# A transformer mixer's three branches laid out in a new order: low-rank tile first, fourteen rounds of inverse, heads and gate tiles

## What is computed

```python
h = rms_norm(x, mix_norm[l])
p = h @ w_in[l]
p_rwkv = token_shift(p[..., :SHIFT_COLS], shift_mu[l])
p_fox = p[..., SHIFT_COLS:SHIFT_COLS + FOX_COLS]
gates = jax.nn.sigmoid(p[..., SHIFT_COLS + FOX_COLS:])
gate_a, gate_b = gates[..., :D_MODEL], gates[..., D_MODEL:]
y_a = rwkv7_mixer(p_rwkv, ...) @ rwkv_proj[l]
y_b = fox_mixer(p_fox, ...) @ fox_proj[l]
x = x + (gate_a * y_a + gate_b * y_b) @ w_out[l]
```

## Time and profile before

| | |
|---|---|
| median of 3 runs | 2981.29 us (2980.33 to 2991.32) |
| profiled execution | 2975.66 us, span 2973.9 us |
| TensorE busy | 2758.8 us (93%) |
| VectorE busy | 1886.0 us (63%) |
| ScalarE busy | 1244.0 us (42%) |
| GpSimd busy | 779.5 us (26%) |
| mean granted clock of TensorE | 0.962 of full |

### The profile page before, as it was taken

One profiled execution on the slowest core, in us unless ns is written; L12 is line 12 of the kernel. 1 busy time (PEld: TensorE's weight loads), 2 busy tenths in 40 slices (PEclk: granted clock), 3 DMA queues, 4 the chain that ended last, 5 costly groups with the idle time before them and its releaser, 6 DMA issues.

```text
span 2973.9 us, 43682 instructions
## 1 busy us (share of the span) xinstructions
PE 2758.8 (93%) x17592; PEld 2495.1 (84%) x17592; DVE 1886.0 (63%) x3243; ACT 1244.0 (42%) x1739; POOL 779.5 (26%) x340
## 2 busy tenths in 40 slices
PE   8989999999999988699999999999799857898998
PEld 7869999999888866599999988888798746776896
DVE  5655997776555566659977765555654675415554
ACT  4434453333444444444633344444444512132443
POOL 0000987664000001029966630000000230042000
PEclk9999999999999999899999999999899978889999
DMA  6554554445666643255544455665456410023454
GB/s 203 161 183 148 171 179 151 139 142 160 192 193 191 192 151 113 79 177 175 172 157 138 141 177 191 191 191 191 135 185 191 127 59 24 1 85 104 159 183 144
DMA packets 122888, 449.49 MB, mean 151 GB/s; under 512 B 13712, under 2 KB 13840, under 8 KB 122560
## 3 DMA queue, kind: packets, MB, share of 16 engines
q1 hardware_dynamic: 120800, 439.47, 46.4%
q0 software_dynamic: 1888, 7.23, 0.7%
HBM read 445.60 MB, written 1.05 MB: 150 GB/s over the span
## 4 chain that ended last, share of the span: by engine, by line
PE 82%; DVE 13%; ACT 2%; POOL 2%; issue 1%; DMA 1%; DVEq 0%; SPq 0%; ACTq 0%
PE ps L428 11%; PE ps L429 11%; PE ps L430 11%; PE ps L478 11%; PE ps L480 11%; PE ps L479 10%; DVE W L1294 10%; PE ps L547 4%; PE ps L676 2%; PE ps L450 2%; PE ps L452 2%; PE ps L451 2%; DVE x L1294 1%; POOL lo L1957 1%; PE ps L414 1%
## 5 line engine op out<-in xcount | busy, mean ns | idle before, releaser
L912 ACT ACTIVATE hi<-ring 128x1024 fp32r<-128x1024 f32 x830 | 878.6, 1059 | 1256.6 <-PE ps L430 649.2
L1317 DVE TENSOR_TENSOR lo<-ring,hi 128x1024 fp32r<-128x1024 f32 x540 | 660.8, 1225 | 583.8 <-ACT hi L912 583.5
L428 PE MATMUL ps<-xT_r,hi 128*128 128x256 f32 x3248 | 935.5, 288 | 12.0 <-POOL lo L1957 8.1
L429 PE MATMUL ps<-xT_r,hi 128*128 128x256 f32 x3248 | 920.8, 284 | 0.0
L430 PE MATMUL ps<-xT_r,lo 128*128 128x256 f32 x3248 | 920.4, 283 | 0.0
L1957 POOL TENSOR_TENSOR lo<-ring,hi 128x1024 fp32r<-128x1024 f32 x290 | 733.5, 2537 | 654.6 <-ACT hi L912 654.6
L428 PEld LDWEIGHTS ps<-xT_r,hi 128*128 128x128 f32 x3248 | 625.0, 192 | 16.1 <-POOL lo L1957 5.5
L429 PEld LDWEIGHTS ps<-xT_r,hi 128*128 128x128 f32 x3248 | 625.5, 193 | 0.7 <-issue 0.7
L430 PEld LDWEIGHTS ps<-xT_r,lo 128*128 128x128 f32 x3248 | 624.9, 192 | 0.0
L478 PE MATMUL ps<-hi,oht_r 128*128 128x512 f32 x1040 | 408.4, 393 | 13.0 <-DVE W L1294 13.0
L480 PE MATMUL ps<-hi,oht_r 128*128 128x512 f32 x1040 | 410.4, 395 | 0.0
(11 more groups left out here) (216 smaller groups left out, 2869.0 us busy)
## 6 DMA issues: line engine op xcount, KB each, us to landing
ring<-in_peer_u SPq DMA_DIRECT2D x256, 512.0 KB, 3.6
ring<-in_peer_v SPq DMA_DIRECT2D x256, 512.0 KB, 3.6
ring<-in_f SPq DMA_DIRECT2D x132, 512.0 KB, 3.5
ring<-in_ret_vg SPq DMA_DIRECT2D x32, 512.0 KB, 3.5
ring<-in_peer_q SPq DMA_DIRECT2D x32, 512.0 KB, 3.6
ring<-in_ret_qk SPq DMA_DIRECT2D x16, 512.0 KB, 4.3
ring<-in_ret_out SPq DMA_DIRECT2D x16, 512.0 KB, 4.1
ring<-in_in_shift SPq DMA_DIRECT2D x14, 512.0 KB, 4.3
```

Of the source, the lines that this page charges most:

```text
L428: pe.matmul(o, h, xT[:, k, 0:256], start=k == 0, stop=False)
L429: pe.matmul(o, h, xT[:, k, 256:512], start=False, stop=False)
L912: hid.done(a.activation(hi[m % NH][:, :], ring[j % NR][:, :], ACT.Copy), j)
L1317: lo_v.done(v.tensor_tensor(lo[m % NH][:, :], ring[j % NR][:, :], as32(hi[m % NH][:, :]), ALU.subtract), j)
```

## The change

The three generators and `weave` go; each engine's program of the mixer is written out in one sequence. The pieces:

- The shift tiles come in the order `SHIFT` = 6, 2, 3, 0, 1, 4, 5: low-rank pair first, then k, r and v. The chain (scan, exponentials, reciprocal, keys, block-diagonal operands) stands between the other shift and fox tiles. The reciprocal is cut into two halves. ScalarE takes the squares and the copies into the block-diagonal operands; VectorE multiplies flat 128x1024 operands instead.
- q and k are normalised once per matrix instead of once per 128 tokens (one `pow` of 16 columns on GpSimd for two of 8), their gains go into the copy after the transposes.
- Fourteen rounds (`ROUNDS`): four with the products of one group, ten with a half level of the inverse. Each takes one gate tile (two in the last two), the stages of one or more head turns (rounds 2 to 11), and rounds 4 to 11 one `bdT`. `Vs` stands ahead of the rounds.
- Tiles of `in_fox`, `fx_out`, `rw_out` and every second gate tile are subtracted on VectorE; 8 gate tiles stay on GpSimd (before: 10 fox, 16 gate, 4 and 2 output tiles).
- Two state buffers `M_S`, one multiply for the four decays; `fx_out` is taken in quarter tiles between the steps of the recurrence.
- x is written to memory after the first feed-forward (4 DMAs of 256 KB) so that its place holds the gates `M_gb`, and read back (4 DMAs) behind the last `w_out` load.

```diff
 PEER_A0 = 69
+SHIFT = (6, 2, 3, 0, 1, 4, 5)
+ROUNDS = 14
...
@@ -84,17 +87,18 @@
         add("f1_13", i)
     for i in range(22):
         add("f1_2", i)
-    for i in range(14):
-        add("in_shift", i)
+    for i in SHIFT:
+        for j in range(2):
+            add("in_shift", 2 * i + j)
     for i in range(12):
-        add("in_fox", i, "V" if i < 2 else "P")
+        add("in_fox", i)
     for name in ("in_ga", "in_gb"):
         for i in range(8):
-            add(name, i, "P")
+            add(name, i, "P" if i % 2 else "V")
     for i in range(4):
-        add("fx_out", i, "P")
+        add("fx_out", i)
     for i in range(4):
-        add("rw_out", i, "P" if i < 2 else "V")
+        add("rw_out", i)
     for i in range(8):
         add("w_out", i)
     for i in range(44):
...
+        M_ga, M_gb = M_vBD.rearrange("p u n -> p (u n)").rearrange("p (a d) -> p a d", a=2), x
+        M_sc = M_LT
+        M_S = [z.rearrange("p (c v) -> p c v", c=4) for z in (M_sc[:, 0:256], M_X[:, 1024:1280])]
+        M_R, M_SA = (M_sc[:, o:o + 256].rearrange("p (c v) -> p c v", c=4) for o in (256, 512))
         M_Y = M_sc[:, 1024:2048]
         M_pC = sm[:, 104:120]
...
+
+        def fox_turn(n):
+
+            return [(n // 4, n % 4)] if 0 <= n < 8 else []
+
+        def gate_count(n):
+
+            return 2 if n >= ROUNDS - 2 else 1
 
         EXP_TILE, PICK_TILE = (25, 53), (32, 58)
...
+                                yield
                     mm.done(ins, "eaten", i)
                     if k < len(tiles) - 1:
                         yield
...
+                def products(g):
+                    for name, l, r in (("LT", M_bBD, M_aBD), ("X0", M_aBD, M_bBD), ("MT", M_kBD, M_aBD), ("BT", M_bBD, M_rBD),
+                                       ("KT", M_kBD, M_rBD)):
+                        prod((name, g), lambda i: l[:, i, :], lambda i: r[:, i, :], g)
+
+                def half_step(k):
+                    lev = k // 2
+                    for g in groups(k):
+                        pe.wait_ge(*at(dve, "CT", lev, g))
+                        prod(("T1", lev, g), lambda i: uh(M_CT, i), lambda i: un(M_X, i), g)
+                    if k < 8:
+                        z, g = k // 4, k % 4
+                        b = bank("bdT", z, g, among=RW)
+                        for j in range(4):
+                            ins = pe.transpose(b[:, j * 128:j * 128 + 128], (M_bBD, M_kBD)[z][:, g * 4 + j, :], ident)
+                        mm.done(ins, "bdT", z, g)
+
+                def full_step(k):
+                    lev = k // 2
+                    for g in groups(k):
+                        pe.wait_ge(*at(act, "T1", lev, g))
+                        if lev < 4:
+                            prod(("dX", lev, g), lambda i: un(M_XT, i), lambda i: uh(M_T1, i), g)
+                        prod(("dXT", lev, g), lambda i: uh(M_T1, i), lambda i: un(M_XT, i), g)
+
+                def scores(tt, hp):
+                    kw = 128 * (tt + 1)
+                    b = bank("fox_s", tt, hp, among=(6,))
...
+                for n in range(ROUNDS):
+                    for w in fox_turn(n - 4):
+                        weights(*w)
+                    if n < 4:
+                        products(n)
+                    else:
+                        half_step(n - 4)
+                    for _ in range(gate_count(n)):
+                        next(tiles)
+                    for w in fox_turn(n - 4):
+                        outputs(*w)
+                    if n >= 4:
+                        full_step(n - 4)
+                    for w in fox_turn(n - 2):
+                        if n == 2:
+                            for z in ("fox_q", "fox_k"):
+                                pe.wait_ge(*at(dve, z, "Tn", 0))
+                                pe.wait_ge(*at(act, z, "Tn", 2))
+                            pe.wait_ge(*at(dve, "fox_cum"))
+                        scores(*w)
...
+                output = mat_out_steps("fx_out", [TILE["fx_out", i] for i in range(4)], lambda k: M_oT[:, k, :],
+                                       lambda k: [at(dve, "fox_oT", "Tl", 2)] if k == 0 else [], among=LATE, fine=True)
...
+                shift_tile(2, 0)
+                for name in ("w_up", "a_up", "g_up"):
+                    v.wait_ge(*at(act, name, 2))
+                ts_(M_lgd, M_lgd, -math.exp(-0.5), None, ALU.mult)
+                step(v.tensor_tensor_scan, M_Lc, M_rst, M_lgd, 0.0, ALU.mult, ALU.add)
+                shift_tile(2, 1)
+                tt_(M_eP, M_Lc, M_lgd, ALU.subtract, name=("decay",))
+                shifted(2)
+                shift_tile(3, 0)
+                for c in range(4):
+                    ts_(c4(M_kk)[:, c, :], k_[:, c, :], pc("kk", c), None, ALU.mult)
+                shift_tile(3, 1)
+                shifted(3)
+                shift_tile(4, 0)
+                for c in range(0, 4, 2):
+                    v.wait_ge(*at(mm, "kk2", c))
+                    ts_(c4(M_kn)[:, c:c + 2, :], j2(ps("kk2", c)), 1e-24, None, ALU.max, name=("kk_norm", c))
+                    empties(dve, "kk2", c)
+                shift_tile(4, 1)
+                shifted(4)
+                shift_tile(5, 0)
+                v.wait_ge(*at(act, "kk_norm"))
+                step(v.reciprocal, M_kn[:, 0:512], M_kn[:, 0:512])
+                shift_tile(5, 1)
+                step(v.reciprocal, M_kn[:, 512:1024], M_kn[:, 512:1024])
+                shifted(5)
+                shift_tile(6, 0)
+                tt_(M_kn, M_kn, M_kk, ALU.mult)
+                keys(0)
+                keys(1)
+                shift_tile(6, 1)
+                keys(2)
+                keys(3)
+                shifted(6)
+                fox_tile(0)
+                for c in range(4):
+                    stt_(c4(M_tmp)[:, c, :], r_[:, c, :], pc("rk", c), c4(M_kk)[:, c, :], ALU.mult, ALU.mult, name=("rk",))
...
+                def corner(k):
+
+                    lev = k // 2
+                    if k:
+                        v.wait_ge(*at(mm, "T1", (k - 1) // 2, groups(k - 1)[1]))
+                    for g in groups(k):
+                        tt_(v8(h2(M_CT, g)), v8(g4(M_LT, g)), mm8(4 + lev), ALU.mult, name=("CT", lev, g))
+
+                def joined(k):
+                    lev = k // 2
+                    for g in groups(k):
+                        v.wait_ge(*at(mm, "dXT", lev, g))
+                        if lev < 4:
+                            tt_(g4(M_X, g), g4(M_X, g), ps("dX", lev, g), ALU.add)
+                            empties(dve, "dX", lev, g)
+                        tt_(g4(M_XT, g), g4(M_XT, g), ps("dXT", lev, g), ALU.add, name=("XT", lev, g))
+                        empties(dve, "dXT", lev, g)
+
...
+                for n in range(ROUNDS):
+                    if n < 4:
+                        products(n)
+                    elif n > 4:
+                        joined(n - 5)
+                    if 3 <= n < ROUNDS - 1:
+                        corner(n - 3)
+                    for w in fox_turn(n - 3):
+                        scores(*w)
+                    for w in fox_turn(n - 3):
+                        weights(*w)
+                    for _ in range(gate_count(n)):
+                        next(tiles)
+                joined(ROUNDS - 5)
...
+                    if n < 3:
+                        S, S_next = M_S[n % 2], M_S[(n + 1) % 2]
+                        bv = ps("dS", n)[:, 0:256].rearrange("p (c v) -> p c v", c=4)
+                        dv = b3(decay[:, n], [128, 4, 64], 2)
+                        v.wait_ge(*at(mm, "dS", n))
+                        if n:
+                            tt_(S_next, S, bv, ALU.add)
+                            tt_(S_next, S_next, dv, ALU.mult, name=("state", n))
+                        else:
+                            step(v.tensor_copy, S_next, bv)
+                            tt_(S_next, S_next, dv, ALU.mult, name=("state", n))
+                        empties(dve, "dS", n)
+                    split(TILE["fx_out", n] + 1)
+                    centre(n)
+                    if n:
+                        spread(n - 1)
+                spread(3)
+                split(TILE["fx_out", 3] + 2)
+                for g in range(2):
...
+            load("fox", [(M_wf, A["in_f"])])
+            load("masks", [(M_mkp, A["mtab"])])
             p.wait_ge(*at(dve, "mix", "Tl", 6))
             for i in range(5):
                 pool.done(p.memset(M_BD[i], 0.0), "zero_bd")
-            weave([mixer_rwkv(), mixer_fox(), mixer_gates()])
+            for z in range(2):
+                power(M_rr[:, z * 16:z * 16 + 16], "fox", z)
+            split(TILE["in_gb", 7])
+            for i in range(4):
+                power(sm[:, 80 + i * 4:84 + i * 4], "lnx", i)
             power(rs_r, "rms", ("ffn", 2))
...
+            def aside(quarter):
+
+                tt, half = quarter // 2, slice(quarter % 2 * 512, quarter % 2 * 512 + 512)
```

(83 more changed lines are left out.)

934 lines of the change are left out of this document (371 added, 563 removed).

## The result

| | before | after |
|---|---|---|
| median | 2980.81 us (2975.55 to 2991.32, 4 runs) | 2909.36 us (2907.84 to 2910.83, 4 runs) |
| profiled execution, span | 2975.66, 2973.9 us | 2910.83, 2908.9 us |
| ratio of the times | | 0.9756, 95% interval 0.9729 to 0.9783 |

The kernel is 71.4 us faster by the medians, 65.0 us by the profiled spans. The forecast was 2900.4 us: inside the range, 9 us too low. The sum of the stages tells more than the total, so here are the changed kernel's stages, from the first shift tile: to the first inverse product, to the end of the last dXT, the last join with the recurrence, the tail to `yT`, and the rest. The first event, the first inverse product, `yT` and the end are the same as in the earlier trace rows; the cuts between them follow the new order. The columns are those of the earlier trace rows.

A forecast was written before the change was run, and what follows sets the result against it. The mixer was taken as bound by waits at the seams of three branches. Its stages summed to 370.7 us against 451.6, 80.9 less, and 2981.3 - 80.9 gave 2900.4 us; range 2885 to 2930.

The forecast's parts named there:

- stage 1: From the first shift tile to the first inverse product: 97.6 us of TensorE work plus 11.5 of waits and slow products, 109.1.
- rounds: Stage 2, fourteen rounds of inverse, heads and tiles: 147.6 us of TensorE work plus 12.0 of waits, 159.6.
- recurrence: Stage 3, four chunks of R, SA, dS and Y with quarter output tiles: 32.6 us at clock 1.00.
- wait for the first fox tile: In stage 1, the first fox tile's `lo` comes 3.4 us after TensorE asks, later ones every 4 to 5 us.
- wait between rounds 3 and 4: At round 4's start TensorE waits 2.9 us for the first head pair's weights, plus 1.5 of slow products.
- other 7.6 us of short waits: In the rounds: 2 us in rounds 0 to 2 and 5.6 spread over ten short waits for bank or join.
- rival (A): Rounds bound by waits: ten with 2.5 us of waiting and 1.5 of slow products, 40 us, total 2940; chance 0.17.
- taking the subtractions off GpSimd would gain nothing: In the rounds, eight gate tiles left on GpSimd block VectorE 16 us, priced at nothing for the path.
- my own rule at the top: On TensorE in the old inverse: a 4.78 us wait is paid twice, as idle time and as slow products behind it.
- (B): Stage 1 bound by VectorE throughout: each of 24 tiles 0.8 us late, 19 us, total 2919; chance 0.10.
- (C): Clock stays low in the rounds: at 0.50 throughout, 139 us more, total 3039; chance 0.02.
- (D): Whole mixer: the new order changes nothing that counts, total 2975 to 2985 us; chance 0.02.

The follow-up runs named there:

- d_turn: Changed kernel with the transposes of the heads' output moved into the two waits of chunk 0, SA instead of R waiting for the last join; median 2882.43 us.
- g_clump: Changed kernel with all sixteen gate tiles in round 0 and none in rounds 1 to 13; median 2924.42 us.
- gate_vec: d_turn with all sixteen gate subtractions on VectorE, none on GpSimd; ratio 0.9692 to the kernel before the change, rounds 160.0 us.
- a_beside: Changed kernel with three 128x512 products ahead of R and three ahead of Y in chunk 0, both 0.57 us waits kept; ratio 0.9686 to the kernel before.
- fox_pool: d_turn with ten of the twelve fox subtractions back on GpSimd; ratio 0.9735 to the kernel before the change, stage 1 115.6 us.
- a_waits: Changed kernel with three 128x512 products in each of the two short waits of chunk 0; ratio 0.9709 to the kernel before, recurrence 33.0 us.
- a_narrow: Changed kernel with seven 64-column products in each of the two short waits of chunk 0; ratio 0.9715 to the kernel before, recurrence 34.7 us.
- b_late: Changed kernel with three 128x512 products ahead of each recurrence group in chunks 1 to 3 only; ratio 0.9730 to the kernel before, recurrence 45.2 us.

## Why the prediction was right, and where it was off

| term | predicted | measured |
|---|---|---|
| stage 1 | 109.1 | 102.0 |
| rounds | 159.6 | 156.5 |
| last join | 1.8 | 1.1 |
| recurrence | 32.6 | 59.0 (33.0 in d_turn) |
| tail | 5.2 | 6.0 |
| from `yT` | 62.4 | 60.8 |
| sum | 370.7 | 385.5 |

**Stage 1.** The work was sized rightly (97.6, busy 96.6 us). The wait for the first fox tile came where I had put it, 3.19 us against 3.4. Behind it I had every lo late until the chain's end; only two more were, by 1.08 and 0.37 us. VectorE was busy 81.7 us against my 79. Part of the gain needed the subtractions moved off GpSimd: with ten of them back, 13.6 us in this stage and 5.9 in the rounds return. That was under the change's first stage in my sum, but with no price of its own. No run takes back the new tile order or the woven chain; that these removed the waits of 11.29 and 17.81 us is read from the two traces alone.

**Rounds.** The work was right: 147.6 us, and 154.0 busy of which 13.7 at half clock, so 147.2 at full clock. A wait between rounds 3 and 4 was there, 2.2 us against 2.9, but at another handover: I had TensorE wait for the first head pair's weights at the start of round 4; it waited at the end of round 3, before the second pair's scores, for VectorE to read the first pair's out of bank 6. The sixteen passes behind took 3.24 us instead of 1.95. The other 7.6 us of short waits did not occur. Slow passes I had priced behind waits only, at 1.5; the four spells cost 6.8 us. g_clump bears on rival (A): even without the tiles between, the rounds grew by 13.5 us, not by 40. That taking the subtractions off GpSimd would gain nothing holds (gate_vec).

**Recurrence.** This term failed. The step was stage 3's "Sum 32.6" at prices of clock 1.00, taken from a chunk of the kernel before, which lay between whole gate tiles of twelve wide products. I had written down the two bare copies of ScalarE in chunk 0 (0.75 each) and priced them as idle time only, though my own rule at the top was that a wait is paid twice. Even by that rule I would have had some slow passes behind them, not 55.86 us. The instructions were sized right, as d_turn shows with 33.0; the clock was not. It cost 26.4 us.

**Rivals.** (B) did not occur: TensorE waited 5.1 us in the stage. (C) named the right loss, a clock that stays at 0.50, in the wrong stage. The Trainium skill ("TensorE: Matmul & The Clock Gate", A second HAM failure mode: psum-queue depth-cycling) tells of small idles between groups with the clock swinging between its levels. In the rounds the clock did swing, through four spells, at a price of 6.8 us and not of 139. In chunk 0 two small waits did bring it down, but then it did not swing: it stayed at 0.50 while TensorE had no idle time at all. (D) did not occur. The sum was 14.8 us too low: 26.4 too little for the recurrence, 11.6 too much for the rest. The forecast missed the median by 9.0 only, because the 5.6 us that I had added for the scale of the medians did not show: the changed kernel's median lies 1.5 us under its profiled execution.

That the time fell inside the range was therefore partly luck, since two errors of opposite sign met. With the recurrence at full clock, as in d_turn, the median is 2882.43 us, below the range's lower end of 2885. Of the signs that I had named, the rounds (156.5 us at 0.96) and the idle time before them (5.4 us) came as said; the first inverse product came at 2420.53 instead of 2426, and `yT` at 2643.22 instead of 2626, which points at the recurrence.

## What to carry to other kernels

Price a short wait by what stands around it: two waits of 0.57 us were harmless with wide products beside them (a_beside) and cost 26 us among 64-column products alone. After a reordering, look for stretches where the tensor engine is busy all the time at a clock of 0.50, since no list of waits shows them; here, filling or flanking the last waits before the stretch repaired it, best with work that must be done anyway. And ask of each filler where it is needed most: with all sixteen gate tiles in one block the rounds lose 13.5 us, while the recurrence lost 26 for want of 1.1 us of work in two places. When a stage grows with its idle time unchanged, as in gate_vec and fox_pool, look at the clock before blaming the engine that was given more work.

## What the runs showed of the hardware that I had not expected

The granted clock depends on what came before as well as on the work. The mix of chunks 1 to 3 (narrow products with three wide ones between the groups) ran at 1.00 to its end where chunk 0 had kept 1.00 (a_waits, a_narrow, d_turn), and in the changed kernel, where chunk 0 had fallen, it stayed at 0.50 to its end, busy without a gap. In b_late the clock came back behind six wide products in a row. And in the rounds it fell four times, to 0.50 for 13.7 us in all, with TensorE busy, at places that differ between two traces of the same instructions.
